# Forget gates, stage ends, the opening and the pieces of the modulation moved in an eight-stage transformer kernel

## The chip, the cores and the metric

The kernel runs on one core (one NeuronCore) of a Trainium2 chip. The engines are TensorE (PE, matmuls), VectorE (DVE), ScalarE (ACT), GpSimd (POOL, here almost only issuing DMAs) and SyncE (SP, issuing DMAs). The metric is the device time of one execution in microseconds, less is better.

## The reference

Two blocks work on x of 256 tokens and 1024 channels, in fp32. Every sublayer normalises x, scales and shifts it by a modulation of the condition c, and adds its result times a gate:

```python
mod = c_act @ ada_w[l] + ada_b[l]                       # first block: 6 x 1024 columns
h = rms_norm(x, norm1_g[l]) * (1 + scale1) + shift1     # q, k, v, p, two gates = h @ w_in
x = x + gate1 * (merged @ w_out[l])                     # attention over 8 heads, and a pool
u = causal_dwconv(h2 @ w_up[l], conv_w[l], conv_b[l])   # second sublayer, 3 taps
x = x + gate2 * ((jax.nn.silu(u_g) * u_v) @ w_down[l])
...
for layer in range(DEPTH_2):                            # second block, 2 layers, 9 x 1024 columns each
    x = x + 0.5 * mod[:, 0, 2][:, None, :] * swiglu(h, ffn_w13[layer, 0], ffn_w2[layer, 0])
    y = swa_mixer(...) if layer % 2 == 0 else fox_mixer(...)   # 16 heads of 64
    x = x + mod[:, 1, 2][:, None, :] * y
    x = x + 0.5 * mod[:, 2, 2][:, None, :] * swiglu(h, ffn_w13[layer, 1], ffn_w2[layer, 1])
```

The sliding-window attention (swa) has 16 query heads on 4 key heads, a window of 128, a table of biases and a sink. The last attention (fox) has forget gates, one number per token and head from 16 more columns of the input product:

```python
log_f = jax.nn.log_sigmoid(fl + b_f)
F = jnp.transpose(jnp.cumsum(log_f, axis=1), (0, 2, 1))
s = s + Fq[..., None] - F[:, :, None, :]
```

## The kernel before, in words

The eight sublayers are eight stages: moba (the first attention, with the pool), conv, ffn, swa, ffn, ffn, fox, ffn. In the windows below they begin at about 0, 237, 431, 633, 761, 964, 1171 and 1342 us, moba with the opening ahead of it until the first product.

**Weights.** They come in 215 units of 1 MB (128 partitions x 2048 fp32). SP loads them into five slots `raw`. An fp32 product is three matmuls at reduced precision: hi x hi, lo x hi and hi x lo. So ACT copies each unit to `hi` (L504) and DVE subtracts to get `lo` in the place of raw (L926, `split_to`, `split_through`). PE waits for `lo_ready`, multiplies, and `unit_done` frees the slot. Activations are split alike: `split_h` makes `h_hi` (L961) and `h_lo` (L963).

**Modulation.** The rows c_act @ ada_w are worked out on DVE beside the products: 48 chunks of 512 columns, 4 of them in the opening, the others as pieces, four per chunk. A piece is a load of 512 KB by POOL (L461) into one of two buffers `ada` and two operations of DVE on 128x512 (L885, L888), which add up in `ada_sum`. When a chunk's four pieces are done, `sums` has PE sum over the partitions by four matmuls with a vector of ones (L1342), and `columns` on DVE adds the bias (L910, `modc`) and for a scale the gain (L915, `acol`). `gate_rows` turns the gate's columns to rows on PE (L1354), and ACT copies them to `gate` (L563). `CHUNKS_IN` says how many chunks each stage works out for later use, and the tables `PIECES_AT`, `SUMS_AT`, `COLS_AT` and `GATES_AT` at which unit each step stands; in swa some pieces stand between the steps of attention instead.

**Order.** Each engine's program is written out by hand and every dependence is a semaphore; nothing is reordered at run time. At the start of a stage `boundary` on DVE does, for each half t of the tokens (128 each), `residual`, `root` (1/rms) and `split_h`, with `split_to(n)` between them, which does all lo parts up to unit n with the pieces that the tables place among them. On ACT it is the squares, the root, `normed` (L532) and after PE's transposes `turn_x` (L1362) `modulated` (tn, L544).

**Attention.** Queries and keys are made in blocks of 512 columns: `block_rows` on PE, `block_square` (ACT), `block_sums` (DVE), `block_root` (ACT, a Sqrt, L638), `block_norm` (DVE, L1037 and L1044), `turn_block` (PE, L1553), `block_evict` (ACT). `attention_step(s, t)` is one step of a pipeline over heads: logits of head t (L1578 or L1583), their maximum (DVE), Exp (ACT, L662), the turning and the values of earlier heads. Sqrt and Exp use different tables of ACT, so a root between two steps brings table loads. In swa the last two blocks, 4 and 5, are made inside the steps.

**Forget gates.** Each product has a part of h as the held operand and 16 moving columns (A[0][:, 16t:16t+16], L1305 to L1307, 48 matmuls). Bias, log sigmoid and cumulative sum follow in `fz`; the sum over tokens is three matmuls with a triangle and ones (L1797 to L1799). `f_parts` (L1275 to L1282) goes to DRAM and back as rows (L471, L475) to be added to the logits.

## Time and profile before

| | us |
|---|---|
| median of three runs (1527.5, 1535.44, 1540.94) | 1535.44 |
| profiled execution | 1542.21 |
| its span | 1540.4 |
| PE busy | 1454.9 (94%) |
| DVE busy | 1055.7 (69%) |
| ACT busy | 732.5 (48%) |
| POOL busy | 140.4 (9%) |

A row of a timeline names the start, the length, the engine, the line of the kernel, the operation, what it writes from what it reads, and in brackets how long the engine stood idle before it and what ended that. Consecutive alike instructions are one row with their count. The granted clock of PE is a share of full speed.

### The profile page before, as it was taken

What the parts mean: (1) busy time and instruction counts of PE and PEld (TensorE: products, weight loads), DVE (VectorE), ACT (ScalarE), POOL (GpSimd) and SP (SyncE); (2) the same over time, 40 slices, a digit from 0 to 9 for tenths busy, and PEclk for the clock granted to TensorE, in tenths of its full rate; (3) what the DMA queues carried; (4) which work ended last, traced back from release to release, by engine and by line L of the source; (5) the groups of instructions that cost most, each with busy time, mean ns of one, the idle gap of its engine ahead of it and who ended that gap; (6) DMA issues with size and microseconds to landing.
All of it is one profiled execution on the core that took longest, in us unless ns stands there. A gap on an engine that the chain in (4) does not pass through costs nothing.

```text
span 1540.4 us, 18813 instructions
## 1 busy us (share of the span) xinstructions
PE 1454.9 (94%) x7463; PEld 1208.0 (78%) x7463; DVE 1055.7 (69%) x1498; ACT 732.5 (48%) x1036; POOL 140.4 (9%) x199
## 2 busy tenths in 40 slices
PE   3799988999999999988999999999999899999998
PEld 2688978999978888765688878788877776688886
DVE  5768866988977777667577777776767346466444
ACT  2554445444564433765544335633337466554432
POOL 1011100110001111000011110011110100000000
PEclk9999999999999999985999999999999799999999
DMA  9677664777759888361478886788863442376552
GB/s 322 236 227 244 233 220 163 267 252 242 250 180 313 284 284 301 113 218 55 156 244 299 289 265 221 235 300 291 288 224 117 133 144 75 105 239 201 170 189 81
DMA packets 192395, 333.94 MB, mean 217 GB/s; under 512 B 8834, under 2 KB 132494, under 8 KB 192308
## 3 DMA queue, kind: packets, MB, share of 16 engines
q1 hardware_dynamic: 164464, 236.02, 45.6%
q0 software_dynamic: 27264, 96.49, 19.6%
q8 instruction: 60, 0.98, 0.3%
q10 hardware_dynamic: 580, 0.23, 0.1%
q14 instruction: 27, 0.22, 0.0%
HBM read 331.55 MB, written 1.15 MB: 216 GB/s over the span
## 4 chain that ended last, share of the span: by engine, by line
PE 67%; DVE 8%; ACT 5%; issue 3%; DMA 2%; ACTq 0%; DVEq 0%
PE bank L1411 9%; PE bank L1413 9%; PE bank L1412 9%; PE bank L1374 7%; PE bank L1376 6%; PE bank L1375 6%; DVE lo L926 3%; PE bank L1305 2%; PE bank L1307 2%; PE bank L1306 2%; PE bank L1539 2%; DMA ada<-in_ada_w 2%; DVE ada_sum L888 2%; PE bank L1342 2%; PE bank L1540 2%
## 5 line engine op out<-in xcount | busy, mean ns | idle before, releaser
L926 DVE TENSOR_TENSOR lo<-raw,hi 128x2048 fp32r<-128x2048 f32 x215 | 490.8, 2286 | 88.0 <-ACT hi L504 87.3
L504 ACT ACTIVATE hi<-raw 128x2048 fp32r<-128x2048 f32 x215 | 405.4, 1909 | 34.4 <-DMA raw<-in_w_out 13.9
L1411 PE MATMUL bank<-hi,h_hi 128*128 128x512 f32 x704 | 279.3, 397 | 2.6 <-DVE lo L926 1.8
L888 DVE SCALAR_TENSOR_TENSOR ada_sum<-ada,c_act,ada_sum 128x512 f32<-128x512 f32 x312 | 234.1, 750 | 65.2 <-DMA ada<-in_ada_w 56.7
L1413 PE MATMUL bank<-hi,h_lo 128*128 128x512 f32 x704 | 275.4, 391 | 0.0
L1412 PE MATMUL bank<-lo,h_hi 128*128 128x512 f32 x704 | 275.2, 391 | 0.0
L461 POOL DMA_DIRECT2D ada<-in_ada_w x176 | 125.3, 712 | 1105.8 <-DVE ada_sum L888 1090.4
L1374 PE MATMUL bank<-hi,o_hi 128*128 128x512 f32 x504 | 205.5, 408 | 8.6 <-DVE lo L926 7.6
L1376 PE MATMUL bank<-hi,o_lo 128*128 128x512 f32 x504 | 197.9, 393 | 0.0
L1375 PE MATMUL bank<-lo,o_hi 128*128 128x512 f32 x504 | 197.5, 392 | 0.0
L611 ACT ACTIVATE KT<-bank 128x256 f32<-128x256 f32 x88 | 33.8, 384 | 322.7 <-PE bank L1413 322.6
L1411 PEld LDWEIGHTS bank<-hi,h_hi 128*128 128x128 f32 x704 | 133.0, 189 | 32.6 <-DVE lo L926 3.5
L1413 PEld LDWEIGHTS bank<-hi,h_lo 128*128 128x128 f32 x704 | 132.8, 189 | 28.6
L1412 PEld LDWEIGHTS bank<-lo,h_hi 128*128 128x128 f32 x704 | 133.0, 189 | 26.5
L1305 PE MATMUL bank<-h_hi,hi 128*128 128x256 f32 x480 | 139.0, 290 | 1.0 <-DVE lo L926 1.0
L1306 PE MATMUL bank<-h_lo,hi 128*128 128x256 f32 x480 | 136.7, 285 | 0.0
L1307 PE MATMUL bank<-h_hi,lo 128*128 128x256 f32 x480 | 136.7, 285 | 0.0
L1374 PEld LDWEIGHTS bank<-hi,o_hi 128*128 128x128 f32 x504 | 95.4, 189 | 31.2 <-DVE lo L926 10.6
L1376 PEld LDWEIGHTS bank<-hi,o_lo 128*128 128x128 f32 x504 | 95.2, 189 | 21.2
L1375 PEld LDWEIGHTS bank<-lo,o_hi 128*128 128x128 f32 x504 | 95.7, 190 | 17.4
L1305 PEld LDWEIGHTS bank<-h_hi,hi 128*128 128x128 f32 x480 | 93.0, 194 | 3.0 <-issue 2.5
L1306 PEld LDWEIGHTS bank<-h_lo,hi 128*128 128x128 f32 x480 | 93.1, 194 | 0.2
(206 smaller groups left out, 1875.3 us busy)
## 6 DMA issues: line engine op xcount, KB each, us to landing
ada<-in_ada_w POOLq DMA_DIRECT2D x176, 512.0 KB, 5.3
raw<-in_ffn_w SPq DMA_DIRECT2D x176, 512.0 KB, 5.4
raw<-in_ffn_w SPq DMA_DIRECT2D x44, 1024.0 KB, 6.3
raw<-in_w_up SPq DMA_DIRECT2D x22, 1024.0 KB, 5.1
raw<-in_w_in SPq DMA_DIRECT2D x16, 1024.0 KB, 7.4
raw<-in_fox_w_in SPq DMA_DIRECT2D x12, 1024.0 KB, 5.1
raw<-in_w_down SPq DMA_DIRECT2D x11, 1024.0 KB, 5.2
raw<-in_swa_w_in SPq DMA_DIRECT2D x6, 1024.0 KB, 5.2
```

The costliest lines, as they stand in the source:

```text
L504: nc.scalar.activation(hi[:, n % NS, :], raw[:, n % NS, :], ACT.Copy).then_inc(hi_ready, 1)
L888: nc.vector.scalar_tensor_tensor(acc, in0=src, scalar=c_act[:, col:col + 1], in1=acc, op0=ALU.mult, op1=ALU.add).then_inc(ada_step, 1)
L926: nc.vector.tensor_tensor(lo[:, n % NS, :], raw[:, n % NS, :], hi[:, n % NS, :].bitcast(F32), ALU.subtract).then_inc(lo_ready, 1)
L1305: mm(outp, wh, xh, start=start, stop=False, skip_group_check=True)
L1306: mm(outp, wh, xl, start=False, stop=False, skip_group_check=True)
L1307: return mm(outp, wl, xh, start=False, stop=stop, skip_group_check=True)
L1374: mm(outp, xk_hi, wh[:, k, cut], start=start, stop=False, skip_group_check=True)
L1375: mm(outp, xk_hi, wl[:, k, cut], start=False, stop=False, skip_group_check=True)
L1376: ins = mm(outp, xk_lo, wh[:, k, cut], start=False, stop=stop, skip_group_check=True)
L1411: mm(bank[:, :], xk_hi, wh[:, i, :], start=k == 0, stop=False, skip_group_check=True)
L1412: mm(bank[:, :], xk_hi, wl[:, i, :], start=False, stop=False, skip_group_check=True)
L1413: ins = mm(bank[:, :], xk_lo, wh[:, i, :], start=False, stop=k == KD - 1, skip_group_check=True)
```

## The change

What it does:

- The opening's four chunks come as eight contiguous pieces of 128x2048, summed by DVE in `pro_sum` in one operation each; 16 one-column matmuls with one columns step follow at the end, where four groups of four stood among the pieces.
- `CHUNKS_IN` is [6, 7, 11, 0, 9, 9, 0, 2] for [6, 6, 9, 3, 9, 9, 0, 2]: swa's pieces and sums are gone, conv has one chunk more and the third stage two. In moba the columns steps stand one unit earlier.
- The forget gates' product holds the weights, zero-padded to 128 columns, and moves 256 tokens: 24 matmuls. Everything after it works on 16x256, and the cumulative sum is a scan on DVE. `f_parts` no longer stands behind `split_through(s, 6)`.
- The output units of moba wait for two merges (the first two units) or four, where the gates and all units waited for four. In conv the transposes of t = 1 stand behind the first products of t = 0, DVE's root before `split_to(2)`.
- In swa the Sqrt of blocks 4 and 5 is one instruction in step 3, and both are normed in step 4, evicted in steps 5 and 6 and turned there.

The core of the diff:

```diff
-CHUNKS_IN = [6, 6, 9, 3, 9, 9, 0, 2]
+CHUNKS_IN = [6, 7, 11, 0, 9, 9, 0, 2]
...
-        at = [3 + (p0 * 27 // (4 * n0) if n0 > 4 else p0) for p0 in range(4 * n0)]
...
+        from0, over = (2, 26) if n0 > 10 else (3, 27)
...
+        for c0 in range(n0):
+            for p0 in range(4 * c0, 4 * c0 + 4):
+                u0 = from0 + (p0 * over // (4 * n0) if n0 > 4 else p0)
+                if c0 > 1:
+                    u0 = max(u0, at_sums[c0 - 2])
+                PIECES_AT[w0 + u0] = PIECES_AT.get(w0 + u0, 0) + 1
...
-        COLS_AT.update({w0 + u: 1 for u in (11, 13, 15, 18, 20, 23)})
+        COLS_AT.update({w0 + u: 1 for u in (10, 12, 14, 17, 19, 22)})
...
-                        if t == 0:
-                            block_root(s, 4)
-                        elif t == 2:
-                            block_evict(s, 4)
+                        if t == 2:
                             block_square(s, 5)
                         elif t == 3:
-                            block_root(s, 5)
-                        elif t == 5:
-                            block_evict(s, 5)
+                            block_roots(s, 4)
+                        elif t in (5, 6):
+                            block_evict(s, t - 1)
...
-                split_to(W0[b] + 2)
-                root(b, 1)
+                if KINDS[b] == "conv":
+                    root(b, 1)
+                    split_to(W0[b] + 2)
+                else:
+                    split_to(W0[b] + 2)
+                    root(b, 1)
...
+                if i == 0:
+                    nc.vector.tensor_scalar(pro_sum[:, :], pro[i], c_act[:, 0:1], None, ALU.mult).then_inc(pro_step, 1)
+                else:
+                    dve.wait_ge(pro_step, i)
+                    nc.vector.scalar_tensor_tensor(pro_sum[:, :], in0=pro[i], scalar=c_act[:, i:i + 1],
+                                                   in1=pro_sum[:, :], op0=ALU.mult, op1=ALU.add).then_inc(pro_step, 1)
...
                         if t in (0, 3):
                             block_sums(s, 4 + t // 3)
-                            block_norm(s, 4 + t // 3)
+                        elif t == 4:
+                            block_norm(s, 4)
+                            block_norm(s, 5)
...
+                    dve.wait_ge(lf_ready, 1)
+                    nc.vector.tensor_tensor_scan(fz[:, 5, :], ones[0:16, 0:1].to_broadcast([16, T]), fz[:, 4, :], 0.0,
+                                                 ALU.mult, ALU.add).then_inc(cum_done, 1)
                     block_sums(s, 3)
                     block_norm(s, 3)
-                    split_through(s, 6)
...
                     if t == 0:
                         take(w)
-                        if u:
-                            turn_x(s, 1)
+                    elif u == 0:
+                        turn_x(s, 1)
...
-                last = SUMS_LAST[kind]
-                if last:
-                    pe.wait_ge(olo_done, (HEAD0[s] + HEADS[kind]) // 2)
-                    sums(1)
                 step_out(s, 3, 0)
-                sums(last // 2)
...
                     if t == 0:
                         take(first + o)
+
+                        pe.wait_ge(merged, 2 if o < 2 else 4)
                     elif o == 3:
                         turn_x(s + 1, 0)
+                    if o == 0:
+                        pe.wait_ge((merge_a, merge_b)[t], 4)
...
+            pe.wait_ge(pro_step, KD)
+            for i in range(2 * KD):
+                ins = mm(M[:, i:i + 1], pro_sum[:, P * i:P * (i + 1)], ones[:, 0:1], start=True, stop=True)
+            ins.then_inc(ada_used, PRO_CHUNKS)
...
-                    pe.wait_ge(merged, 4)
                     out_units(s, h_hi, h_lo)
...
+                    held = lambda w, k: w[:, k:k + KD, :].rearrange("p a b -> p (a b)")
+                    for k in range(KD):
+                        ins = product(A[0][:, 0:T], held(f_hi, k), held(f_lo, k), h_hi[:, k, :], h_lo[:, k, :],
+                                      k == 0, k == KD - 1)
                     ins.then_inc(fl_done, 1)
                     block_rows(s, 1, 1, 0, 4)
                     turn_block(s, 0)
                     block_rows(s, 1, 1, 4, KD)
                     turn_block(s, 1)
-
-                    pe.wait_ge(lf_ready, 1)
-                    lf = fz[:, 4, :]
-                    mm(A[1][0:16, 0:P], lf[:, 0:16], tri, start=True, stop=True)
-                    mm(A[1][0:16, P:T], lf[:, 0:16], ones[:, :], start=True, stop=False)
-                    mm(A[1][0:16, P:T], lf[:, 16:32], tri, start=False, stop=True).then_inc(cum_done, 1)
```

DVE at the start of the third stage (the first ffn), from the lo part of its second unit on. L926 is that subtraction, L885 and L888 are pieces, L954 the root of the second half, L961 and L963 its split. Before:

```order
L926 TENSOR_TENSOR lo<-raw_49,hi 128x2048 [waits hi_ready]
L954 RECIPROCAL rms<-rms 128x1 [waits std_ready]
L926 TENSOR_TENSOR lo<-raw_49,hi 128x2048 [waits hi_ready]
L885 TENSOR_SCALAR ada_sum<-ada,c_act 128x512 [waits ada_used,ada_full0]
L888 SCALAR_TENSOR_TENSOR ada_sum<-ada,c_act,ada_sum 128x512 [waits ada_step]
L888 SCALAR_TENSOR_TENSOR ada_sum<-ada,c_act,ada_sum 128x512 [waits ada_step,ada_full1]
L888 SCALAR_TENSOR_TENSOR ada_sum<-ada,c_act,ada_sum 128x512 [waits ada_step]
L961 CAST h_hi<-tn 128x4x128 [waits hf_ready]
L963 TENSOR_TENSOR h_lo<-tn,h_hi 128x4x128 [waits hhi_ready]
```

And with the change (L936, L895, L898, L964, L971 and L973 are the same lines):

```order
L936 TENSOR_TENSOR lo<-raw_49,hi 128x2048 [waits hi_ready]
L895 TENSOR_SCALAR ada_sum<-ada,c_act 128x512 [waits ada_used,ada_full0]
L898 SCALAR_TENSOR_TENSOR ada_sum<-ada,c_act,ada_sum 128x512 [waits ada_step]
L898 SCALAR_TENSOR_TENSOR ada_sum<-ada,c_act,ada_sum 128x512 [waits ada_step,ada_full1]
L898 SCALAR_TENSOR_TENSOR ada_sum<-ada,c_act,ada_sum 128x512 [waits ada_step]
L964 RECIPROCAL rms<-rms 128x1 [waits std_ready]
L936 TENSOR_TENSOR lo<-raw_49,hi 128x2048 [waits hi_ready]
L898 SCALAR_TENSOR_TENSOR ada_sum<-ada,c_act,ada_sum 128x512 [waits ada_step,ada_full0]
L898 SCALAR_TENSOR_TENSOR ada_sum<-ada,c_act,ada_sum 128x512 [waits ada_step]
L898 SCALAR_TENSOR_TENSOR ada_sum<-ada,c_act,ada_sum 128x512 [waits ada_step,ada_full1]
L898 SCALAR_TENSOR_TENSOR ada_sum<-ada,c_act,ada_sum 128x512 [waits ada_step]
L971 CAST h_hi<-tn 128x4x128 [waits hf_ready]
```

Two pieces now stand ahead of the root and two more, which need both buffers loaded again, ahead of the split of h.

PE at the end of the first attention stage. L1354 (later L1379) turns the second gate's columns, L1374 to L1376 (later L1399 to L1401) are the products of the first output unit. Before:

```order
L1354 MATMUL bank6<-kon,modc 128x128 [waits gate_ready,mod_ready,merged]
L1354 MATMUL bank6<-kon,modc 128x128 x3
L1374 MATMUL bank0<-hi,h_hi 128x512 [waits lo_ready]
L1375 MATMUL bank0<-lo,h_hi 128x512
L1376 MATMUL bank0<-hi,h_lo 128x512
```

And with the change:

```order
L1379 MATMUL bank6<-kon,modc 128x128 [waits gate_ready,mod_ready]
L1379 MATMUL bank6<-kon,modc 128x128 x3
L1399 MATMUL bank0<-hi,h_hi 128x512 [waits merge_a,merged,lo_ready]
L1400 MATMUL bank0<-lo,h_hi 128x512
L1401 MATMUL bank0<-hi,h_lo 128x512
```

The wait for merged has moved from the gates to the first product, and it is now for two merges, not four.

## Rows read from the trace of the kernel before

**Rows 1.** Windows by stage: start:end length, busy of PE, PEld, DVE, ACT, POOL, clock, DMA, GB/s.

```profile
65.00:237.00 172.00, 160.57 (x1065) 144.29 (x1064) 126.52 (x214) 81.17 (x122) 18.18 (x25) 0.95 0.70 227
237.00:431.00 194.00, 190.56 (x1355) 180.13 (x1355) 161.30 (x218) 94.61 (x109) 17.06 (x24) 0.99 0.69 228
431.00:633.00 202.00, 200.25 (x953) 166.06 (x952) 151.03 (x168) 91.92 (x105) 25.57 (x36) 1.00 0.81 267
633.00:761.00 128.00, 115.19 (x490) 80.96 (x489) 82.07 (x210) 73.77 (x172) 8.52 (x12) 0.83 0.39 130
...
1171.00:1342.00 171.00, 162.54 (x720) 120.82 (x719) 81.66 (x185) 99.51 (x186) 4.29 (x7) 0.92 0.33 109
```

**Rows 2.** Timeline of the opening: start, length, what it is, idle before it.

```profile
38.24 1.91 ACT L504 ACTIVATE hi<-raw 128x2048 fp32r<-128x2048 f32 x1 [3.80 <-DMA raw<-in_w_in]
...
40.68 1.84 PE L1342 MATMUL bank<-ones,ada_sum 128*128 128x1 f32 x8 [3.59 <-DVE modc L910]
...
46.33 0.77 PE L1539 MATMUL bank<-hi,h_hi 128*128 128x512 f32 x1 [3.81 <-DVE h_lo L963]
```

**Rows 3.** Grouped lines, whole span: count, busy us, mean ns, idle before.

```profile
L926 DVE TENSOR_TENSOR lo<-raw,hi 128x2048 fp32r<-128x2048 f32 x215 | 490.8, 2286 | 88.0 <-ACT hi L504 87.3
...
L888 DVE SCALAR_TENSOR_TENSOR ada_sum<-ada,c_act,ada_sum 128x512 f32<-128x512 f32 x312 | 234.1, 750 | 65.2 <-DMA ada<-in_ada_w 56.7
...
L963 DVE TENSOR_TENSOR h_lo<-tn,h_hi 128x512 fp32r<-128x512 f32 x32 | 22.2, 692 | 1.1
```

**Rows 4.** Timeline of the first attention stage.

```profile
149.30 1.84 PE L1342 MATMUL bank<-ones,ada_sum 128*128 128x1 f32 x8 [2.55 <-DVE modc L910]
...
163.57 2.29 DVE L926 TENSOR_TENSOR lo<-raw,hi 128x2048 fp32r<-128x2048 f32 x1 [1.72 <-ACT hi L504]
...
202.52 2.08 PE L1354 MATMUL bank<-kon,modc 128*128 128x128 f32 x8 [4.46 <-DVE h_lo L1149]
...
206.95 0.45 PE L1374 MATMUL bank<-hi,h_hi 128*128 128x512 f32 x1
```

**Rows 5.** Timeline of the start of the conv stage.

```profile
236.77 1.94 PE L1362 MATMUL bank<-kon,work 128*128 128x128 f32 x8 [4.42 <-ACT work L532]
```

**Rows 6.** Timeline of the third stage.

```profile
449.73 0.50 PE L1411 MATMUL bank<-hi,h_hi 128*128 128x512 f32 x1 [0.29 <-DVE h_lo L963]
...
467.68 0.72 POOL L461 DMA_DIRECT2D ada<-in_ada_w  x1 [10.13 <-DVE ada_sum L888]
...
474.12 1.54 DVE L888 SCALAR_TENSOR_TENSOR ada_sum<-ada,c_act,ada_sum 128x512 f32<-128x512 f32 x2 [2.75 <-DMA ada<-in_ada_w]
```

**Rows 7.** DMA issues of the page: count, KB each, us from issue to landing.

```profile
ada<-in_ada_w POOLq DMA_DIRECT2D x176, 512.0 KB, 5.3
```

**Rows 8.** Waits in the third stage: us in total, times, longest.

```profile
DVE ada_sum L888 <- DMA ada<-in_ada_w: 16.1, 11, 3.9
```

**Rows 9.** Timeline of the sliding-window stage.

```profile
678.76 1.28 ACT L638 ACT_TABLE_LOAD   x1
...
680.38 0.20 DVE L1037 RECIPROCAL hstd<-hstd 128x8 f32<-128x8 f32 x1 [3.40 <-ACT hstd L638]
...
752.67 1.05 PE L1342 MATMUL bank<-ones,ada_sum 128*128 128x1 f32 x8 [0.93 <-DVE o_lo L1081]
```

**Rows 10.** Windows of 4 us (columns as in group 1) in the two attentions of the second block.

```profile
689.00:693.00 4.00, 3.98 (x13) 2.18 (x12) 2.17 (x10) 3.15 (x9) 0.00 (x0) 0.50 0.00 0
...
1199.00:1203.00 4.00, 4.00 (x16) 3.68 (x16) 0.00 (x0) 0.00 (x0) 0.00 (x0) 0.50 0.00 0
```

**Rows 11.** Timeline of the last attention stage.

```profile
1193.89 0.17 PE L1305 MATMUL bank<-f_hi,h_hi 128*128 128x16 f32 x1
...
1201.21 0.77 PE L1539 MATMUL bank<-hi,h_hi 128*128 128x512 f32 x1
...
1215.67 0.60 PE L1797 MATMUL bank<-kon,fz 128*16 128x128 f32 x2 [5.06 <-DVE fz L1269]
...
1222.11 0.40 DVE L1275 CAST f_parts<-bank 16x256 fp32r<-16x256 f32 x1
```

More of the change, by code:

```diff
@@ L639, in block_root, with block_roots @@
                                      scale=1.0 / HD).then_inc(bstd_ready, 1)
+            def block_roots(s, e):
+                act.wait_ge(bsum_done, N0[s] + e + 2)
+                nc.scalar.activation(hstd[:, :, :], hstd[:, :, :], ACT.Sqrt, bias=eps[:, 0:1],
+                                     scale=1.0 / HD).then_inc(bstd_ready, 2)
             def block_evict(s, e):
                 act.wait_ge(bt_done, N0[s] + e + 1)
+                if s == 0 and e == 0:
+                    act.wait_ge(bias_out, 32)
                 dst, gain = normed_to(s, *NORMED[KINDS[s]][e])
@@ L1092, in attention_step @@
                     out_lo(s, (t - 3) // 2)
-                columns(int(t in COLS_STEP[kind]))
-                pieces(int(t in PIECES_STEP[kind]))
             def step(ins):
@@ L1241, in _ @@
                     block_norm(s, 3)
-                    pieces(2)
                     dve.wait_ge(bias_in, 32)
@@ L1627, in attention_step @@
                     values(s, t - 3)
-                sums(int(t in SUMS_STEP[KINDS[s]]))
             def step_out(s, o, t):
@@ L1704, in _ @@
             pe.wait_ge(ones_set, 1)
-            sums(1)
             pe.wait_ge(small_full, SMALL_LOADED)
```

114 lines of the change are left out of this document (54 added, 60 removed).

## The prediction

> **What bounds the kernel now.** I read the windows by stage first [rows 1], then the timeline around every place that the diff touches, then the grouped lines for prices. The profiled execution took 1542.2 us for a span of 1540.4, 1.8 outside it. TensorE (PE) is busy 1454.9 us of it. In the plain feed-forward stages it is busy 200.25 of 202 us: nothing is to be had there but fewer instructions. The reader should see in [rows 1] the two attention stages: busy 115.19 of 128 us and 162.54 of 171, with a mean granted clock of 0.83 and 0.92 of 2.4 GHz (half clock below is 1.2 GHz). So PE's time there is lost twice, by waits and by matmuls at half clock. The first attention stage loses 11.4 of 172 us to waits. Behind PE stands VectorE (DVE): each 1 MB weight unit costs it 2286 ns (the lo part), each piece of the modulation two operations of 750 ns [rows 3]. In the conv stage it is busy 161.3 of 194 us.
>
> **The opening.** Before, PE's eight last sums take 1.84 us from 40.68; the first product starts at 46.33, held by h_lo, not by the weights: the first unit's hi, that waited for its load, starts at 38.24 [rows 2]. The change has DVE do 8 operations of 2048 columns for 32 of 512. No row has that shape; from lo at 2048 columns (2286) against h_lo at 512 (692) [rows 3], 1536 more columns cost 1594 ns, so such an operation takes about 750 + 1594 = 2344, the eight 18.8 us instead of 24.0. But the pieces themselves come over the same DMA engines, ahead of the weights that land only at 38.24, so not all of the 5.2 comes through: I take the last operation to end some 3 us earlier, between nothing and 5. Against it: the sums no longer run beside the pieces. All 32 records stand behind the last piece, 7.4 us at the price of the eight of [rows 2] (0.23 each) against 1.84, +5.5; one combined columns step saves about 1.2 us of round trips. Sum -3 + 5.5 - 1.2 = **+1.3**, bounds -2 and +3.
>
> **The first attention stage.** The columns step moves one unit earlier. In [rows 4] PE waits 2.55 us for modc at 149.30 and its sums then run 1.84 us, the half-clock price. That goes, but DVE is nearly full there: a wait for hi of 1.72 us at 163.57 [rows 4] and another of about 1 are the slack that can give way, and what PE gains beyond it is lost again to lo: **-2.8**. At the stage's end the gates no longer wait for all four merges. PE idled 4.46 us before 202.52 and ran at half clock until 206.95 [rows 4]. After: the gates start at 198.1, eight of them cost 1.1 us at full clock, the first output unit then has both banks free and two merges done; lo of the second unit (DVE 202.38 to 204.67 before) meets PE at about 204.8, just in time. The product that began at 204.25 begins at 199.2 (-5.05), and the stretch 204.25 to 206.95 at full clock gives 1.3 more; 0.3 I leave to the one late lo: **-6.6** with the clock. Bounds of both together -12 and -5. Sum here about -9.5.
>
> **The conv stage.** Before, PE waits 4.42 us for the normed half at 236.77, and the transposes sit between the first products of t = 0 [rows 5]. The change lets both units' t = 0 run first, so PE works during that wait. But DVE has to deliver h(t = 1) before the next product: two lo (2.29 each) and now two pieces (3.0, one of them more than before) stand ahead of split_h, and ACT's tn stands behind another hi of 1.9. I get h at about 244 where PE wants it at 240.5, that is a new wait of some 3.5 us and half clock after it, against 4.42 gained: **+3.3**, bounds 0 and +4.5 (upper end: the stall of before plus the extra piece's 1.5, less what overlaps). In the body 4 pieces more, 8 operations, 6 us of DVE, whose free time is 32.7 of 194 us [rows 1]: **+1.5**, bounds 0 and +4.
>
> **The third stage** takes 11 chunks for 9, 44 pieces for 36. DVE goes from 151 to 163 of 202 us, which it can hold. Two things can't be read from that. First the start: before, h for t = 1 came just ahead of 449.73, PE waiting 0.29 us for it [rows 6]. Two pieces (3.0 us) now stand ahead of the root and two more ahead of split_h, and the second pair waits for its reload: **+5**, bounds +3 and +7. Second the pace. There are two buffers, each reloaded when its operations are done. The page gives 5.3 us to landing [rows 7]; with 0.3 to issue and 1.5 of DVE a buffer's turn is 7.1 us, two pieces per turn, 22 turns are 156 us of the 163 that the plan leaves (442.7 to 605). It fits with little to spare; but the load issued at 467.68 held DVE 2.75 us until 474.12 [rows 6], 6.4 us. I take **+3**, bounds 0 and +17 (22 turns of 8.2 are 180).
>
> **The sliding-window stage** loses all its 12 pieces and 3 sums. The two last sums at the stage's end (1.05 us in [rows 9] and one of 0.8) stand on PE's own path: -1.85; the sum in step 1 as well, -1.1. The first pieces at the stage's start held PE some 0.9. Then the merged root: each visit of a Sqrt between the Exps costs two table loads of 1.28 us, and in [rows 9] DVE waits 3.40 us for hstd at 680.38 behind the first of them; one visit less is -2.6 where ACT is on the path. The 8 pieces between the steps cost DVE 12 us, but PE is busy 3.98 of 4 us in 689 to 693, at clock 0.50 [rows 10]: its own instructions set the pace there, and DVE's room is worth little, I say 0.5. -1.85 - 1.1 - 0.9 - 2.6 - 0.5: **-7**, bounds -4 (the root and the start hidden) and -14 (all twelve pieces' time beside the sums).
>
> The Trainium skill, "ScalarE: Activation LUTs", section "What ACT_TABLE_LOAD costs", gives a drain of some 1380 ns beside the 1283 of the load, 2.66 us per switch. By it one visit less would save 5.3 us. The trace has the load at 1.28 and the next ACTIVATE in its place right behind it (678.76 + 1.28 = 680.04; hstd is there at 680.38) [rows 9], so I go by the row.
>
> **The last attention stage.** The 48 forget-gate matmuls take 1193.89 to 1201.21 = 7.3 us [rows 11]; the clock falls to half among them ([rows 10], 1199 to 1203) although PE is busy throughout. Now 24 with 256 columns, 0.12 us each at full clock as the same shape in the trace: 2.9 us, -4.4; the following twelve at full clock, -2.4. Then the wait of 5.06 us at 1215.67, the three cumulative matmuls (1.3 us at half clock) [rows 11] and the half clock behind them until about 1221 (-2.5) go. In their place DVE scans 256 columns of 16 rows in 0.4 to 0.75 us (the nearest rows are the 16 x 256 operations of 0.40, [rows 11]). The forget rows' parts, at 1222.11 before, come at about 1214, and their round trip through DRAM of 7.6 us lands at 1221.4. New waits: turn_block 2 for ACT's evict behind Exp and Ln (1.0), turn_block 3 behind a hi (1.5). -4.4 - 2.4 - 5.06 - 1.3 - 2.5 + 2.5 = **-13**, bounds -16 and -9.
>
> For the scan the Trainium skill, "DVE: opcode table, instruction layouts, handler registers and perf-mode slots", section 6, has half throughput. It would make it 0.75 at most; no row of before shows one.
>
> The stages with 9 chunks stand as before: 0.
>
> **Sum**: +1.3 - 9.4 + 3.3 + 1.5 + 5 + 3 - 7 - 13 = -15.3. The profiled time becomes 1542.2 - 15.3 = 1526.9. The runs' median is 1535.44; the profiled execution stands 6.8 above it. The same shift on the median: **1520 us**.
>
> **Rivals.** (a) *The clock stays high in the sliding-window steps.* With no pieces between steps PE may wait differently; [rows 10] shows half clock at full business, so it hangs on what came before. 128 us at 0.83 [rows 1] lose 22 us to the clock; half of it given back: -10 more, 1510. Against: the waits of 1 us per step stay. (b) *The loads pace the third stage.* If landing takes 6.4 us as in [rows 6] and not 5.3 [rows 7], the body costs +17 instead of +3 and PE waits at most units; each fall of the clock costs some 2.2 us as at 202.52 (4.4 us at half), three of them 6.6: 1520 + 14 + 6.6 = 1541, slower than before. It decides from 6.4 us of landing with the clock falling. For: DVE waits 11 times for these loads there, 16.1 us in all and 3.9 at most [rows 8]; DMA share 0.81 already [rows 1], with 4 MB more to move. Against: in between are 20 units where nothing waits. (c) *The forget rows come too late.* If the round trip starts behind split and norm work, the first logits wait 6 to 8 us: 1527. (d) *The start waits win*: conv and third stage each at their upper end (+1.2 + 2 + 2.5) and the opening at +3: 1527 too, told from (c) only by place.
>
> **How the numbers follow.** The forecast as summed (1514 to 1526): 0.55. (a) 0.15; (b) 0.10; (c) 0.09; (d) 0.11. The range leaves out (b) and the best tail of (a): 1505 to 1533. About 1% (15 us) is what a measurement of this kernel can tell from no change; the forecast stands right on that edge, 1520.1. Faster by more: (a) and just over half of the forecast, 0.45. Slower than 1550.8 only by (b) with more falls: 0.06. The rest within 1%: 0.49.
>
> **What would show it.** Opening: first product at 46 to 49. First attention stage: no wait of 4.5 us ahead of the gates, stage 9 us shorter. Conv: the first wait on h_lo, 3 to 4 us, not on work. Third stage: 5 to 10 us longer, DVE's waits for ada above the 16.1 us of [rows 8]. Sliding window: one Sqrt visit between steps, 7 us shorter. Last attention: 24 gate matmuls in 3 us and no wait on the cumulative sum, 13 us shorter. Wrong it would be above all by the clock: each stretch of half clock that appears or goes is 2 to 10 us, and none of these sums can tell it in advance.

## The result and the profile after

The changed kernel takes 1572.74 us (median of 4 runs, 1567.97 to 1577.62) against 1533.2 for the kernel before (4 runs): ratio 1.0255, interval 1.0195 to 1.0315. It is 40 us slower where 15 us faster were forecast. The profiled execution took 1575.6 us, its span 1573.8. The profiled execution of before, 1542.2 us, lies 9 us above the median of its kernel, so the two traces differ by 33.4 us only.

Where they differ is best read from one instruction that each stage begins with, the reciprocal of DVE for the first half (`RECIPROCAL rms`, L954, later L964). The table is worked out from the start times of these eight rows in each trace and the span:

| stage | before, us | after, us | difference | forecast |
|---|---|---|---|---|
| opening, up to the first root | 29.4 | 36.3 | +6.9 | +1.3 |
| moba | 194.7 | 197.0 | +2.3 | -9.4 |
| conv | 206.6 | 211.4 | +4.8 | +4.8 |
| third (ffn, 11 chunks) | 199.8 | 239.1 | +39.3 | +8 |
| swa | 131.0 | 124.1 | -6.9 | -7 |
| ffn | 201.4 | 201.3 | -0.1 | 0 |
| ffn | 205.4 | 200.9 | -4.5 | 0 |
| fox | 169.1 | 160.7 | -8.4 | -13 |
| last ffn | 203.0 | 203.1 | +0.1 | 0 |

The -4.5 in an unchanged stage is spread: in the eighteen other traces of these kernels that stage takes 200.1 to 203.8 us, so before's 205.4 was a slow one, and no difference of that size in a single trace is a finding.

The stages of the changed kernel as windows, columns as in [rows 1], which they answer:

```profile
65.00:241.00 176.00, 164.64 (x1085) 147.53 (x1084) 126.86 (x216) 79.10 (x118) 18.19 (x25) 0.96 0.69 222
...
447.00:685.00 238.00, 210.90 (x952) 170.33 (x951) 159.91 (x188) 90.34 (x103) 31.26 (x44) 0.96 0.74 242
685.00:809.00 124.00, 112.12 (x473) 78.90 (x472) 67.80 (x184) 72.51 (x173) 0.00 (x0) 0.83 0.25 85
...
1217.00:1376.00 159.00, 151.38 (x672) 110.65 (x671) 80.89 (x183) 96.08 (x180) 4.27 (x7) 0.95 0.33 108
```

The third stage is the one to look at. PE is idle 27 of 238 us there, where it was idle 1.75 of 202. The DMA engines are less busy than before (0.74 against 0.81), and so, as a share, is DVE (160 of 238 against 151 of 202). Nothing is full, so the time went to waits. The waits of that stage (us in total, times, longest) answer [rows 8]:

```profile
DVE ada_sum L898 <- DMA ada<-in_ada_w: 25.4, 14, 2.8
DVE ada_sum L895 <- PE bank L1367: 19.7, 5, 4.3
PE bank L1399 <- DVE lo L936: 10.0, 5, 4.1
PE bank L1447 <- DVE KT L1023: 7.3, 4, 3.3
DVE ada_sum L895 <- DMA ada<-in_ada_w: 6.2, 3, 3.4
PE bank L1436 <- DVE lo L936: 5.5, 4, 4.6
```

DVE waits 31.6 us for pieces and 19.7 us for PE's sum that frees an accumulator. PE then waits for DVE. The timeline shows how the one becomes the other:

```profile
534.33 0.49 DVE L895 TENSOR_SCALAR ada_sum<-ada,c_act 128x512 f32<-128x512 f32 x1 [4.33 <-PE bank L1367]
...
535.90 0.70 POOL L465 DMA_DIRECT2D ada<-in_ada_w  x1 [10.81 <-DVE ada_sum L898]
...
539.98 1.54 DVE L898 SCALAR_TENSOR_TENSOR ada_sum<-ada,c_act,ada_sum 128x512 f32<-128x512 f32 x2 [2.73 <-DMA ada<-in_ada_w]
541.43 2.28 DVE L936 TENSOR_TENSOR lo<-raw,hi 128x2048 fp32r<-128x2048 f32 x1
...
543.77 0.50 PE L1399 MATMUL bank<-hi,o_hi 128*128 128x512 f32 x1 [3.95 <-DVE lo L936]
```

DVE waits 4.33 us for the sum. Since it held both load buffers during that wait, POOL had issued nothing for 10.81 us, so the next piece is 4.1 us away from its issue at 535.90. DVE waits 2.73 us for it, with the lo part behind it in program order, and PE waits 3.95 us for that lo. Both rings are empty at the same moment, and each refill is paid in the open.

The opening with the change, for [rows 2]:

```profile
29.61 1.12 PE L1725 MATMUL bank<-kon,TB 128*128 128x128 f32 x4 [26.36 <-DMA TB<-in_fox_k_g]
...
31.54 2.35 DVE L1180 SCALAR_TENSOR_TENSOR pro_sum<-V,c_act,pro_sum 128x2048 f32<-128x2048 f32 x1
...
41.67 6.98 PE L1738 MATMUL bank<-ones,pro_sum 128*128 128x1 f32 x32 [0.63 <-DVE pro_sum L1180]
...
52.63 0.77 PE L1564 MATMUL bank<-hi,h_hi 128*128 128x512 f32 x1 [3.97 <-DVE h_lo L973]
```

The first product starts at 52.63 in place of 46.33. The small table of norm gains (the last of it is `TB<-in_fox_k_g`) is turned at 29.61, before at 20.51. DVE's step on these columns stands ahead of the last four piece operations, so these start only at 31.54. They take 2.35 us each as estimated, and the 32 records 6.98.

The first attention stage, one row of its middle and then its end (for [rows 4] and [rows 5]):

```profile
179.29 1.87 PE L1367 MATMUL bank<-ones,ada_sum 128*128 128x1 f32 x8 [5.30 <-DVE o_lo L1247]
...
207.12 1.05 PE L1379 MATMUL bank<-kon,modc 128*128 128x128 f32 x8
...
211.98 1.15 POOL L449 DMA_DIRECT2D TB<-bias_by_distance  x1 [25.89 <-DVE h_lo L1161]
...
213.13 1.41 POOL L465 DMA_DIRECT2D ada<-in_ada_w  x2
...
213.69 14.92 SPq L385 DMA_DIRECT2D raw<-in_w_up  x3
...
227.96 1.91 ACT L508 ACTIVATE hi<-raw 128x2048 fp32r<-128x2048 f32 x1 [13.73 <-DMA raw<-in_w_up]
...
234.27 1.97 PE L1387 MATMUL bank<-kon,work 128*128 128x128 f32 x8 [6.06 <-ACT work L536]
```

The 4.46 us wait ahead of the gates is gone, and they run at full clock (8 in 1.05 us). But the second weight unit of conv is now issued at 213.69, just behind 3 MB that POOL issued at 211.98 and 213.13 (the 2 MB table of biases for the next attention and two pieces). It lands at 227.96, 14.3 us later. ACT has that unit's hi ahead of conv's squares in its program, so the first half of x, ready at 224.3 (DVE's last residual on it starts at 223.58), waits for a weight that PE doesn't need yet.

The first row is the other half of this stage's story. The columns steps stand one unit earlier, and PE's wait for `modc` (2.55 us at 149.30 before) is gone. But PE now waits 5.30 us for `o_lo` at the sums that come next, where it waited for nothing before.

The last attention stage (for [rows 11]):

```profile
1235.49 0.28 PE L1331 MATMUL bank<-h_hi,f_hi 128*128 128x256 f32 x1
...
1251.03 0.68 DVE L1296 TENSOR_TENSOR_SCAN ada<-ones,ada 16x256 f32<-16x256 f32 x1
...
1254.15 0.27 DVE L1301 CAST f_parts<-ada 16x256 fp32r<-16x256 f32 x1
...
1266.09 0.46 PE L1608 MATMUL bank<-KT,QT 64*128 64x128 f32 x2 [2.22 <-DMA f_rows<-forget_rows]
```

The 24 matmuls start 0.12 us apart, 2.9 us in all, and the scan costs 0.68. From the stage's root to the first logits it is 56.1 us against 67.3 before (1168.3 to 1235.6), with the wait of 2.22 us for the forget rows in it: their round trip takes 10.2 us (issued at 1255.87, there at 1266.09). The attention steps behind take 104.6 us against 101.8, at a mean granted clock of 0.92 against 0.95.

### The profile page after: what moved, and what is told of

It reads as the page before. It is cut to its first block, busy times and chain, and to the rows that moved or that the text cites. A ratio compares the mean times of both kernels' runs of the same rounds, so it can differ in the third digit from the quotient of the medians.

```text
span 1573.8 us, 18725 instructions
## 1 busy us (share of the span) xinstructions
PE 1453.6 (92%) x7433; PEld 1201.7 (76%) x7433; DVE 1052.3 (67%) x1473; ACT 728.8 (46%) x1033; POOL 139.9 (9%) x198
## 4 chain that ended last, share of the span: by engine, by line
PE 69%; DVE 11%; DMA 9%; ACT 6%; issue 3%; ACTq 1%; POOL 0%; SPq 0%; DVEq 0%; POOLq 0%
PE bank L1436 8%; PE bank L1438 8%; PE bank L1437 8%; PE bank L1399 7%; DMA ada<-in_ada_w 6%; PE bank L1401 6%; PE bank L1400 6%; DVE ada_sum L898 4%; DVE lo L936 4%; PE bank L1331 3%; PE bank L1332 3%; PE bank L1333 3%; PE bank L1564 2%; PE bank L1566 2%; PE bank L1565 2%
## 5 line engine op out<-in xcount | busy, mean ns | idle before, releaser
L936 DVE TENSOR_TENSOR lo<-raw,hi 128x2048 fp32r<-128x2048 f32 x215 | 490.8, 2286 | 71.3 <-ACT hi L508 70.8
L898 DVE SCALAR_TENSOR_TENSOR ada_sum<-ada,c_act,ada_sum 128x512 f32<-128x512 f32 x308 | 231.2, 751 | 74.9 <-DMA ada<-in_ada_w 66.6
L1399 PE MATMUL bank<-hi,o_hi 128*128 128x512 f32 x504 | 207.4, 411 | 18.7 <-DVE lo L936 16.7
L1401 PE MATMUL bank<-hi,o_lo 128*128 128x512 f32 x504 | 199.6, 396 | 0.0
L1399 PEld LDWEIGHTS bank<-hi,o_hi 128*128 128x128 f32 x504 | 96.8, 192 | 42.7 <-DVE lo L936 20.6
L1401 PEld LDWEIGHTS bank<-hi,o_lo 128*128 128x128 f32 x504 | 96.1, 191 | 21.5
L1400 PEld LDWEIGHTS bank<-lo,o_hi 128*128 128x128 f32 x504 | 96.8, 192 | 17.7
```

What stands on the lines that cost most here:

```text
L898: nc.vector.scalar_tensor_tensor(acc, in0=src, scalar=c_act[:, col:col + 1], in1=acc, op0=ALU.mult, op1=ALU.add).then_inc(ada_step, 1)
L936: nc.vector.tensor_tensor(lo[:, n % NS, :], raw[:, n % NS, :], hi[:, n % NS, :].bitcast(F32), ALU.subtract).then_inc(lo_ready, 1)
L1399: mm(outp, xk_hi, wh[:, k, cut], start=start, stop=False, skip_group_check=True)
L1400: mm(outp, xk_hi, wl[:, k, cut], start=False, stop=False, skip_group_check=True)
L1401: ins = mm(outp, xk_lo, wh[:, k, cut], start=False, stop=stop, skip_group_check=True)
```

## The experiments

Every ratio is against the kernel before, run on the same chip in turn, with its 95% interval. All edits are to the kernel before unless said otherwise.

**1. Forget gates and the one root together (gates_roots).** The two parts of the diff as printed.

> The kernel before with two parts of the change alone: the forget gates (24 held products, the scan on DVE) and in the sliding-window stage the one root for blocks 4 and 5; pieces, opening and stage ends as before. Theory (each part is worth what its stage shows): the last attention stage ends 13 us earlier, the sliding-window stage 1 to 4 us, so 1516 to 1520 us against 1533, ratio about 0.99. Rival (the gain of 13 us in the changed kernel's last attention came with something else, such as another phase of the weight loads): less than 6 us in all.

Measured: 1525.63 us, ratio 0.9948 (0.9922 to 0.9975), -7 us by the medians. That is less than the theory; the interval, -4 to -12 us, doesn't tell it from the rival's upper end. In its trace the last attention stage takes 157.6 us.

**2. All of the change but the chunks per stage (no_pieces).** The changed kernel with

```diff
-CHUNKS_IN = [6, 7, 11, 0, 9, 9, 0, 2]
+CHUNKS_IN = [6, 6, 9, 3, 9, 9, 0, 2]
```

and the old formula for the table, with pieces and sums again between the steps of swa.

> The changed kernel with the old share of chunks per stage (6, 6, 9, 3, 9, 9, 0, 2), the old table of pieces and the pieces back inside the sliding-window stage; all else changed. Theory (the third stage lost its 38 us to the 11 chunks): that stage is back at 200 to 204 us, the sliding-window stage 2 to 4 us longer than in the changed kernel, in all 1573 - 38 + 3 = about 1538 us. Rival (what is late at the start of the third stage comes from the conv stage's start, or from weights that come late): the third stage stays over 215 us.

Measured: 1534.83 us, ratio 1.0012 (0.9984 to 1.004). The third stage is back at 199.9 us. So the 38 us of the result are the chunks and their table, and the other parts together cost and give about the same. Their shares can't be added up, though: tested alone below, the opening (+12 by its ratio), both stage ends (+6), the forget gates (-6) and the one root (-1) sum to +11 us, where this run shows +2 (-2 to +6). What makes up these 9 us stays open.

**3. Nine and nine (nine_nine).** The changed kernel with `CHUNKS_IN = [6, 9, 9, 0, 9, 9, 0, 2]`.

> The changed kernel with 9 chunks in conv and 9 in the third stage instead of 7 and 11; nothing else. The sum of pieces ahead of the sliding-window stage is the same. Theory (the table for 11 chunks, not the number of pieces, is what costs: DVE waits there for PE's sum of two chunks before): the third stage is back at about 202 us, conv takes 3 to 8 us more for 8 pieces, in all 1573 - 38 + 6 = about 1541 us. Rival (any two pieces more cost a stage their DVE time or their loads, 8 pieces x 4 us): conv is 20 us or more longer, in all over 1555 us.

Measured: 1543.52 us, ratio 1.0048 (1.0022 to 1.0074). Third stage 205.4 us, conv 220.5 against 211.4 with 7 chunks. The same 72 pieces cost 29 us less when they are spread otherwise, so it isn't their number in the two stages together. Conv paid 9, a little over the theory.

**4. A third accumulator (third_sum), 5. a third load buffer (third_load), 6. both (third_both).** The changed kernel; for the third stage's chunks the tile V, unused there, serves as the third of its kind:

```diff
-                    if c >= PRO_CHUNKS + 2:
-                        dve.wait_ge(ada_used, c - 1)
+                    if c >= PRO_CHUNKS + 2:
+                        dve.wait_ge(ada_used, acc_freed(c))   # c - 2 in the third stage
...
-                acc = ada_sum[:, c % 2, :]
+                acc = ada_acc(c)                              # V[:, 0, 0:512] for every third chunk there
```

```diff
-                        pool.wait_ge(ada_step, 2 * (n - 1))
+                        pool.wait_ge(ada_step, ada_place[n][2])   # the piece that used this buffer last
...
+                    b = ada_place[n][0]
+                    pool.dma_start(ada_third if b == 2 else ada[:, b, :, :], ...).then_inc(ada_full[b], 16)
```

> The changed kernel with a third accumulator for the chunks of the third stage, in an unused tile, so that a chunk's first operation waits for PE's sums of three chunks before, not two. Pieces, loads and their places are the same. Theory (DVE waits for PE's sums, which stand behind weights that DVE has not split yet: 19.7 us of such waits in five places): these waits go and the third stage is 15 to 25 us shorter, about 1553 us. Rival (the two load buffers pace it, 20.2 + 6.2 us of DVE waiting for loads): DVE's waits for loads grow by what the others shrink, and the stage is shorter by less than 5 us.

> The changed kernel with a third buffer for the loads of the third stage's pieces (an unused tile), so that a load is issued a piece earlier; two accumulators and the table as in the changed kernel. Theory (two load buffers pace the stage; the third accumulator alone gave 3 us): DVE's waits for these loads go from 31.6 us to under 10, and the stage is 15 us or more shorter than 239, in all about 1555 us. Rival (the accumulator ring and the buffers are one chain, each hides behind the other): the waits for PE's sums grow by what the waits for loads shrink, and the stage stays above 228 us. Second rival (DVE's own 163 us in lumps of up to three pieces per unit): waits go, the stage stays long.

> The changed kernel with both, the third accumulator and the third load buffer, in the third stage. Theory (buffers and ring together): waits of both kinds nearly gone, the third stage at 205 to 212 us, in all 1540 to 1546 us. Rival (lumps of DVE work): no waits for loads or sums to speak of and still over 222 us, 1556 us or more.

Measured: third_sum 1569.71 us, ratio 1.0235 (1.0193 to 1.0276), third stage 228.1 us; third_load 1548.17, 1.0103 (1.0048 to 1.0158), 212.1 us; third_both 1546.51, 1.0102 (1.0064 to 1.0139), 204.9 us. The waits of the third stage with the third load buffer:

```profile
DVE ada_sum L904 <- PE bank L1377: 16.5, 6, 4.3
PE bank L1409 <- DVE lo L946: 4.4, 4, 1.3
...
DVE ada_sum L904 <- DMA V<-in_ada_w: 1.1, 1, 1.1
...
DVE ada_sum L907 <- DMA ada<-in_ada_w: 0.6, 2, 0.4
```

31.6 us of waiting for loads became 1.7, with the bytes, the table and DVE's work unchanged, and the stage is 27 us shorter: PE is idle 9.8 us, 17 less, and busy 203.2 us, 8 less for the same products, at a mean granted clock of 1.00 in place of 0.96. The waits for sums stay at 16.5, and cost little now: the loads arrive during them. The third accumulator alone takes 11 us off the stage, less than its theory (15 to 25) and more than its rival (under 5). DVE's waits for sums are gone there, and its waits for loads have grown from 31.6 to 40.3 us, which is what the rival said they would do. Its edit has a flaw that shows elsewhere: chunk 29, after the third stage, waits for the sum of chunk 28 rather than 27, and the fifth stage takes 208.8 us (207.5 in third_both) against 198.8 to 202.9 in the traces without the flaw. So read third_both as some 6 us too slow by my edit. The theory of the load buffers held and its rivals fell: it is neither lumps of DVE work nor the accumulators alone. The accumulators are the smaller second part (212.1 to 204.9 us). Even with both, 11 chunks take 5 us more than the 199.9 of 9 chunks and the old table.

**7. The opening alone (opening), 8. with its small columns last (opening_cols), 9. with rows of 2 KB (opening_2k), 10. x loaded earlier in the old opening (x_early).**

```diff
 # opening_cols
             for i in range(6, KD):
                 pro_piece(i)
+            dve.wait_ge(cols_done, 1)          # moved from ahead of piece 4
+            nc.vector.tensor_scalar(cols[:, C_GAIN:C_GAIN + 6:2], ...)
 # opening_2k
-                sp.dma_start(pro[i], a["ada_w"][0][P * i:P * (i + 1), 0:2 * D])
+                for odd in range(2):
+                    part = lambda ap: ap.rearrange("p (a b n) -> p a b n", b=2, n=512)[:, :, odd, :]
+                    sp.dma_start(part(pro[i]), part(a["ada_w"][0][P * i:P * (i + 1), 0:2 * D]))
 # x_early, in the kernel before
-                if i == 5:
+                if i == 3:
```

> The kernel before with the new opening alone (eight contiguous pieces of 128x2048, all one-column sums at the end, x loaded before the fourth). Theory (in the changed kernel the first lo stood 6.3 us later, of it 5 us because PE's 32 records of 7 us stand behind the last piece, and the rest because DVE waits 6.4 us for the small columns): +4 to +7 us, 1537 to 1540. Rival (the late start is made up in the first attention stage, where the weight loads have had more time): within 2 us of before.

> The kernel before with the new opening, and in it DVE's step on the small columns (it waits for them until 31.5 us) moved behind the last piece operation. Theory (the new opening's +10.6 us is half the 32 records at the end and half this wait, which holds four ready pieces): the first lo stands 2 to 5 us earlier than in the opening as changed (49 us), in all 1537 to 1541 against 1543. Rival (pieces 5 to 8 land only at 31 to 39 us anyway, x and the smaller loads being ahead of them): less than 1 us.

> The kernel before with the new opening alone, its pieces loaded in two DMAs each whose rows are 2 KB pieces (columns 0 to 511 and 1024 to 1535, then the others), the same bytes in the same places. Theory (the rows of 8 KB hold back the small loads): the small columns are there at 20 to 24 us as before, the first lo stands 3 to 6 us earlier than 49 to 52, in all 1536 to 1539 against 1543. Rival (x's place, or just the bytes ahead): they land at 29 us or later and the time is 1541 or more.

> The kernel before, with x loaded before the fourth piece and not before the sixth, nothing else. Theory (rows of 8 KB are the cause): the small columns land at 20 to 23 us, x earlier, the time within 2 us of before. Rival (x's place is): the small columns land after 27 us and the kernel is 4 to 8 us slower.

Measured: opening 1543.04 us, ratio 1.0076 (1.0046 to 1.0106); opening_cols 1540.95, 1.0057 (1.0027 to 1.0086); opening_2k 1535.86, 1.0006 (0.9982 to 1.003); x_early 1534.73, 1.0019 (0.9994 to 1.0044). The opening costs 11 to 12 us, more than expected. Moving the columns' step helps little (about 3 us by the ratios, whose intervals overlap), since ACT's squares and roots stand behind the same small load (in opening_cols DVE waits 5.79 us for the root instead). Giving the loads 2 KB rows again takes it back, as far as the runs can tell:

```profile
20.08 1.11 PE L1719 MATMUL bank<-kon,TB 128*128 128x128 f32 x4 [16.61 <-DMA TB<-in_fox_k_g]
...
37.45 5.38 PE L1732 MATMUL bank<-ones,pro_sum 128*128 128x1 f32 x32 [1.20 <-DVE pro_sum L1174]
...
46.81 0.77 PE L1556 MATMUL bank<-hi,h_hi 128*128 128x512 f32 x1 [3.98 <-DVE h_lo L971]
```

The small table is there at 20.08 (32.83 in the run with rows of 8 KB), the first product at 46.81 (55.85 with rows of 8 KB; 44.0 to 46.8 in the eleven traces with the old opening). x's place does nothing to the small table (20.36), and its run, some 3 us above before with an interval that holds 0, is nearer to its theory (2) than to the rival (4 to 8). The old opening loads each piece in one DMA with rows of 2 KB, so it isn't the number of DMAs either.

**11. Both stage ends (ends), 12. the first attention's end alone (moba_end), 13. the same with the table of biases loaded later (moba_end_late_table), 14. conv's start alone (conv_start).** The parts of the diff as printed, and for 13

```diff
             pool.wait_ge(merged, 4)
+            load_pieces(6, PIECES * CHUNKS_IN[0] + 8)   # the first eight pieces of conv
             by_distance(1, 16)
             load_pieces(6)
```

> The kernel before with the stage ends alone: in moba the columns one unit earlier and the waits for two or four merges, in conv the later transposes and the other order of root and normed. Theory (moba's end is really 5 us better, and conv's start 3 us worse because the weight load that ACT waits for shares the queues with the 2 MB table of biases): between -4 and +1 us. Rival (the collision came from the changed kernel's other phase and is not there): -5 us or more, with no wait of more than 8 us of ACT for in_w_up.

> The kernel before with the first attention stage's part alone: columns one unit earlier, the gates without the wait for the merges, the first two output units waiting for two merges. Both stage ends together gave +4.5 us with the conv stage's root 3.8 us later and a wait of ACT of 14.5 us for in_w_up. Theory (output units start earlier, so the second in_w_up load is issued together with the 2 MB table of biases and takes 14 us, not 7; ACT has that unit's hi ahead of conv's squares): the conv stage's root stands 2 to 5 us later than before, the whole 0 to +4 us. Rival (the whole loss of both ends is conv's part): -3 us or better, root at 220 or earlier.

> The same, with the 2 MB table of biases loaded after the eighth piece load of the conv stage and no longer at the end of the first attention stage. Theory: the second in_w_up load takes 6 to 8 us again, ACT's wait for it is under 9 us, the conv stage's root stands at 217 to 220 us in place of 224.1, in all -4 to -7 us against before. Rival (the load is late for another reason, such as the two pieces issued with the table or the slot that comes free late): ACT's wait stays over 12 us and the time as without this edit.

> The kernel before with the conv stage's start alone: transposes of the second half behind the first products of the first, ACT's normed and DVE's root ahead of the next unit's hi and lo. Theory (PE's wait of 4.4 us before the transposes is traded for a wait on h_lo): the conv stage's first h(t = 1) product no earlier than before, +1 to +3 us. Rival (the trade pays when the weights are on time): -2 us or better.

Measured: ends 1537.03 us, ratio 1.0041 (1.0016 to 1.0066); moba_end 1536.33, 1.0026 (0.9998 to 1.0054); moba_end_late_table 1529.41, 0.9978 (0.9957 to 1.0); conv_start 1535.05, 1.0005 (0.998 to 1.003). ACT's waits for this weight at the end of the stage, without and with the later table:

```profile
ACT hi L504 <- DMA raw<-in_w_up: 16.7, 2, 13.2
```

```profile
ACT hi L505 <- DMA raw<-in_w_up: 10.3, 2, 6.8
```

Conv's root stands at 227.1 us, then at 219.2, before at 224.1. The moba end with the table out of the way takes 189.8 us from root to root (189.6 in experiment 17, 191.9 in 18), against 192.7 to 195.9 in the traces with the old opening and the old end: 4 us between the means, of which the runs show 3 to 5 with an interval that just reaches a ratio of 1. The collision with the table made it a loss.

The part has a second half that pays nothing. In all eleven traces with the earlier columns PE's wait for `modc` (2.4 to 3.8 us in the other nine) is gone, and PE waits 4.2 to 5.7 us for `o_lo` at the next sums, which it does in none of the nine. The later waits for the merges stand behind both places in PE's program, so the columns are what is left to cause it; how they do is not shown. No run has the new end with the old place of the columns.

Conv's own part is nothing that these runs can tell from zero: PE's wait of 4.42 us for the normed half is traded for one of 5.72 us for h_lo, at 242.56.

**15. The one root alone (roots), 16. the forget gates alone (gates).**

> The kernel before with one root for blocks 4 and 5 in the sliding-window stage alone, pieces inside the stage as before. Theory (one visit of the Sqrt less, two table loads of 1.28 us, of which about half is on PE's path): -1 to -3 us. Rival (both norms now stand together in step 4 on DVE, 3 us ahead of a normalise step, and take back what the loads give): 0 to +2 us.

> The kernel before with the forget gates' part alone (24 held products, everything on 16x256, the scan on DVE, f_parts ahead of the sixth unit's split). Theory (the last attention stage is 11 to 12 us shorter wherever this part is in): 1534 - 11 = 1521 to 1525 us. Rival (part of it is given back, as gates_roots at -7 in the runs suggests): 1526 to 1529 us.

Measured: roots 1532.49 us, 0.9994 (0.9973 to 1.0016); gates 1528.15, 0.996 (0.9931 to 0.9989). The root's two table loads less are in the trace (3 loads from 674 to 700 us where 5 were), the time isn't: swa takes 128.5 us, within the 127.8 to 131.4 of the traces without that part. The gates give 6 us, with an interval of 2 to 11. To the first logits their trace is 11 us shorter, with this wait in it:

```profile
1217.95 0.76 PE L1586 MATMUL bank<-KT,QT 64*128 64x128 f32 x2 [2.31 <-DMA f_rows<-forget_rows]
```

PE waits 2.31 us for the forget rows, which a slower path used to hide. Then the steps behind run at a mean granted clock of 0.90 (106.0 us to the next root) against 0.95 before (101.8), and 4 of the 11 are gone again. Over all traces, ten with this part and ten without, the stage takes 156.2 to 162.2 us with it and 163.9 to 169.1 without. The stretch up to the first logits is 10.3 us shorter in the mean (clock 1.00 against 0.87 to 0.92), the steps 2.8 us longer (100.1 to 106.0 us at 0.90 to 0.97, against 98.7 to 101.8 at 0.95 to 0.98). Some 2 us of the runs' gain lie elsewhere: in the four traces with the old opening and this part the first product starts at 44.0 to 44.2 us, in the seven without the part at 45.6 to 46.8. No run shows which line of the part does that.

**17. What paid (best), 18. the same with the changed chunks and three buffers of both kinds (best_pieces).** best is the kernel before with the forget gates, the one root, and experiment 13.

> The kernel before with what paid: forget gates, one root for two blocks, the first attention stage's end with the table of biases loaded in the conv stage; opening, conv start and pieces as before. If the parts add up (-7 to -11 for the first two, -5 for the third): 1518 to 1523 us. Rival (they hide behind each other or behind the run's own spread): over 1525.

> The same with the changed chunks per stage (7 in conv, 11 in the third, none in the sliding-window stage) and a third accumulator and load buffer for the third stage. Theory (sliding-window stage -5 to -6 us, third stage +4 to +5, conv +1 to +2): within 3 us of best. Rival (moving the pieces is worth it once the loads have room): 4 us or more below best.

Measured: best 1517.07 us, ratio 0.9888 (0.985 to 0.9926); best_pieces 1530.95, 0.9967 (0.9942 to 0.9992). So best beats both kernels, by 1.1% over before (16.6 us by the medians, where the parts alone sum to 10 to 13: the spread of the medians, or that they help each other, these runs don't tell). best_pieces is 14 us behind best, where its theory said within 3. It has the flaw of third_sum (DVE waits 8.88 us for a sum at 804.45, fifth stage 207.8 us). Without these some 7 us it would still be 7 behind: swa gives 6.7 (124.0 for 130.7), the third stage takes 4.6, conv 1.4; moba, the same in both kernels, takes 2.3 more in this trace, and the last attention stage, the same too, 4.4 (160.6 against 156.2), which is spread.

## Why the prediction was wrong

*Third stage: the term that failed.* "22 turns are 156 us of the 163 that the plan leaves ... I take +3, bounds 0 and +17" measured +39.3 with the start. The start (+5 forecast) was fair: PE waits 3.6 us for h_lo there, once. The body was priced as a pace, as if DVE took each piece when it landed. It doesn't: its program is in order, lo parts, sums' releases and pieces stand in one row, and a buffer is refilled only after its operation. When one thing is late, both buffers stay full, no load is in flight, and the next landing is waited for in the open, with PE's lo behind it. third_load shows that it was this: no byte less, 27 us gone. Nor had I priced the accumulators' ring, two deep too: 8.6 us of waits for PE's sums at 9 chunks, 19.7 at 11. With the changed table a chunk's first piece stands at the very unit of the sum that frees its accumulator, and DVE works ahead of PE. Rival (b) named the loads and the right sign, and reached 1541 us: its price of 6.4 us of landing was wrong, for the 44 loads of this stage landed in 5.3 us at the median, as the 36 did before. It had 0.10.

*Opening: mis-sized by a mechanism that I didn't have.* +1.3, bounds to +3; measured +6.3 at the first product and +11 to +12 us in the runs of the part alone. The terms written down were right (2.35 us per operation, 32 records in 3.9 to 7.0 us, one columns step): opening_2k, which has just these, starts its first product 0.5 us later than before and ends at 1.0006. What was missing is what loads with long rows do to the small loads of another queue.

*First attention stage: -9.4 forecast, +2.3 measured.* Two steps failed. The end's -6.6 (its own terms, -5.05 - 1.3 + 0.3, make -6.05): the wait of 4.46 us went, at full clock, as described, but I followed PE and DVE to the stage's end and not the weight load that POOL's table now meets, 14.3 us in place of 7.4. With the table moved the stage gives some 4. And the columns' -2.8, whose warning ("what PE gains beyond it is lost again to lo") came true beyond its price: the wait of 2.55 us for `modc` went, and one of 4.2 to 5.7 us for `o_lo` came for it.

*Conv* +4.8 and *sliding window* -7 came out to the digit, and largely by luck. Conv's +3.3 for the start doesn't follow from its terms (a new wait of 3.5 against 4.42 gained, and some half clock). Alone, the conv start is +0.8 us in the runs, within their spread, and +1.3 in the stage of its trace; the seventh chunk is +1.4 (best_pieces against best); the remaining 2 us of the changed kernel are unexplained. There both waits stand, 6.06 us on work and 6.91 on h_lo, where the forecast had the first gone and 3 to 4 us for the second. Before's swa trace was one of the slower of its kind. Of swa's gain some 6 us are the pieces and sums, the merged root next to nothing; the sum had 2.6 for it. Alone, the root gave -1 us, with an interval of 3 either way. The 2.66 us per switch of the Trainium skill, "ScalarE: Activation LUTs", section "What ACT_TABLE_LOAD costs", 5.3 for one visit less, are not seen in the trace before: a load of 1.28 us starts at 678.76, 0.02 us behind the end of ACT's instruction ahead of it, and ACT's next one starts at 680.05.

*Last attention stage*: the mechanisms were right (24 matmuls in 2.9 us, no wait for the sum, scan 0.68 us, 11.2 us less to the first logits), the size not: 6 us in the runs against 13. Rival (c) came in small: the forget rows' round trip, taken as 7.6 us, took 10.2, and PE waited 2.22 us for it. And the forecast took half-clock time as gone where part of it was moved: 10.3 us less to the first logits in the mean over the traces, 2.8 more in the steps behind.

## What to carry to other kernels

Where one engine does two kinds of work in order, price a ring (load buffers, accumulators) by what happens when it is empty, not by its mean pace: count the slots, and ask what stands behind the instruction that waits for the refill. One more slot was worth 24 us here, and with it the kernel was still 1% slower than before: it took back a good part of what the 11 chunks had cost. When a step moves earlier, follow the DMAs it releases as far as the next load that somebody waits for, and look at the engine's next waits: one that goes can come back larger a few steps on. And try the parts alone: of this change's five, one and a half paid.

## What the runs showed of the hardware

- Loads with contiguous rows of 8 KB hold back small loads of other queues: the norm gains' columns were turned at 17.7 to 20.5 us in the twelve traces with rows of 2 KB and at 29.4 to 32.8 in the eight with rows of 8 KB, at the same bytes. The profile's page has the counts (packets in all and under 8 KB, before and then after): about 1,000 packets more of 8 KB or over, the eight loads' 1,024 rows.

```profile
DMA packets 192395, 333.94 MB, mean 217 GB/s; under 512 B 8834, under 2 KB 132494, under 8 KB 192308
```

```profile
DMA packets 189290, 333.91 MB, mean 212 GB/s; under 512 B 8834, under 2 KB 132462, under 8 KB 188180
```

- A 1 MB load took 14.3 us when 3 MB had been issued on another queue in the 1.7 us before, and 7.4 at the same place before (211.32 to 218.74).
- A scan over 256 columns of 16 partitions takes 0.68 us, a tensor_tensor of that shape 0.41: the Trainium skill, "DVE: opcode table, instruction layouts, handler registers and perf-mode slots", section 6, has half throughput, and the trace goes that way (0.27 us more for the scan).
- The same attention steps of the last attention stage, unchanged, ran at a mean granted clock of 0.95 to 0.98 of 2.4 GHz in the ten traces with the old forget gates and at 0.90 to 0.97 in the ten with the new ones, 98.7 to 106.0 us for the same instructions.
